# First expert rows of a token written plainly with the residual; no base rows stored, no spare products ahead of the first gathered rows

## The chip, the cores and the metric

The kernel runs on one core of one Trainium2 chip. The metric is device time in microseconds (us) of one execution, as a median of several. Engines: TensorE (PE, with its weight loads shown as PEld), VectorE (DVE), ScalarE (ACT), GpSimd (POOL) and SyncE (SP), whose queue only issues transfers. Sixteen DMA engines carry the transfers of all queues.

## The reference, cut to what matters

One encoder layer on 768 tokens (512 + 256) of width 1024, in fp32. A token mixer gives h; then a mixture of experts is added to it: 32 experts in 4 groups, one group for each token, and two experts of that group.

```
h = x + token_mixer(rms_norm(x))
gp = softmax(x @ w_group_router + b);  g_val, g_idx = top_k(gp, 1)
ep = softmax(el[group g_idx]);         e_val, e_idx = top_k(ep, 2)
gate = g_val * e_val / sum(e_val)
for e in range(32):
    hdn = silu(x @ w_gate[e]) * (x @ w_up[e])
    y = y + combine[:, e:e+1] * (hdn @ w_down[e])
return h + y
```

Here x in the second part is rms_norm(h). Each expert has 3 x 256 x 1024 weights, 3 MB in fp32, so the 32 experts bring 96 MB from memory. Each token has exactly two expert rows, so 1536 rows of 4 KB are gathered and 1536 rows are brought to the output.

## The kernel before

**Projection and routing.** After attention the kernel goes through six tiles of 128 tokens. For each tile TensorE does the output projection, DVE adds the residual (`residual`), which leaves the tile of h in `h_sb`, and the router runs: logits, the two experts (columns 182 and 183 of `route_f`), weights, and the place of each token in the slot list of each expert. Every tile of h is stored twice: by ACT's queue into the table `token_rows`, from which the experts gather (`store_row`), and by SP's queue into the output `out`, as the base to which expert rows are added (`store_h`). Before POOL gathers anything it waits for both. SP's queue issues the loads of the experts' weights between these stores.

**Slots.** For each tile TensorE multiplies a one-hot matrix (`slot_a`) by a table with three blocks of 32 columns (`slot_b`: token number, gate weight, rstd), `slot_product`. This gives for each pair of experts and each slot which token it holds, or a number beyond the last token for an empty slot. The first 64 tokens of an expert lie in block 0 (`idx_all`, `gate_all`), the next 64 in block 1 (`idx_more`, `more_all`).

**Pairs.** Experts j and j+16 make pair j, 0 to 15, with 64 slots each, so 128 rows. For each pair POOL gathers the rows by an indirect DMA (`gather_pair`, two pairs ahead, three buffers `g_rows`), TensorE transposes them, multiplies by gate and up weights (`gate_up`, L884), ACT and DVE make `hid`, TensorE transposes and multiplies by the down weights (`down`, L900), ACT copies one half of the product to `y_sb` and DVE the other half (`y_copy`), and POOL adds the 128 rows to `out` by an indirect DMA that adds at its destination (`add_rows`, L1702). Entries of an empty slot lie out of bounds and move nothing. The next add starts when the one before has landed (`main.added`). The last pair adds two halves of its rows (`add_half`, L1708). An expert with more than 64 tokens needs a further pass on the same weights (`over`, block 1); pair 0 and pair 6 have one each in the profile. Within a pass for `over`, TensorE waits until its product has left the banks before it goes on to the next pair, and POOL waits until its add has landed before it gathers again.

**Weights.** SP's queue keeps three buffers of pair weights (6 MB each) filled (`load_pair`, `refill`): a part of pair j is loaded once pair j-3 has used its buffer (waits on `g_mm`, `gu_mm`, `y_mm`) and the third transfer before it has landed (`part_in`). Pair 3's gate weights have a buffer of their own.

**Ahead of the first pair** TensorE issues 40 products that nobody reads (`keep_clock(40)`, L823), then transposes the first gathered rows (L871).

All pairs run in one order written out by hand on every engine: pairs 0 to 3, a loop over 4 to 12, pairs 13 to 15 (`run_pairs`).

## Time and profile before

| what | value |
|---|---|
| median of 3 runs | 608.5 us (605.67 to 611.92) |
| the profiled execution's own time | 608.44 us |
| its span, first to last instruction | 606.7 us |
| mean granted TensorE clock | 0.967 of 2.4 GHz |
| PE busy / DVE busy / ACT busy / POOL busy | 536.3 / 218.0 / 168.9 / 139.8 us |
| moved by DMA | 140.97 MB |

The time of the execution is 1.7 us more than its span. Busy times are sums over stages with different limits; a matmul counts as busy while it is in the pipeline, so 88% for PE does not say that PE sets the time everywhere. In the profile a transfer's share is given of all sixteen DMA engines together.

### The profile page before, as it was taken

The page shows a single profiled execution, that of the slowest core. Times are in us where ns is not written, and L with a number is a line of the kernel's source. Part 1 is how long each engine was busy: PE and PEld are TensorE (multiplying, and loading weights), DVE is VectorE, ACT ScalarE, POOL GpSimd, SP SyncE. Part 2 cuts the span into 40 slices and gives each one's busy share as a digit, 9 for nine tenths or more (in the row PEclk, how much of TensorE's full clock was granted, in tenths as well). Part 3 has the DMA queues.
Part 4 walks back from the last instruction along what each step waited for, and adds up shares of the span by engine and source line. Part 5 has one row for each costly group of instructions (what it writes and reads, how often), then busy time and mean ns, then how long its engine had stood idle before and what let it go on. Part 6 is the DMA issues. An engine that isn't in the chain of part 4 may idle for free.

```text
span 606.7 us, 9491 instructions
## 1 busy us (share of the span) xinstructions
PE 536.3 (88%) x3304; PEld 393.1 (65%) x3305; DVE 218.0 (36%) x602; ACT 168.9 (28%) x421; POOL 139.8 (23%) x230
## 2 busy tenths in 40 slices
PE   4899999999989999999978888878987699897794
PEld 4888988987557677788867545555644456554451
DVE  4754234333657755427772112202111112211111
ACT  6743343332434333125431201202111012111010
POOL 0232232222503300004535022222211222222212
PEclk9999999999989999999987999999998979998978
DMA  8741000012312111199979689999999999999993
GB/s 339 269 116 36 19 18 1 19 51 77 111 63 97 42 36 36 35 357 421 398 263 303 223 264 368 361 365 378 360 372 384 411 393 375 375 354 382 372 392 56
DMA packets 33458, 140.97 MB, mean 232 GB/s; under 512 B 10489, under 2 KB 11148, under 8 KB 21351
## 3 DMA queue, kind: packets, MB, share of 16 engines
q1 hardware_dynamic: 25776, 124.33, 53.6%
q0 software_dynamic: 5856, 12.60, 8.7%
q10 hardware_dynamic: 1766, 3.25, 1.4%
q8 instruction: 36, 0.59, 0.4%
q14 instruction: 24, 0.19, 0.1%
HBM read 131.15 MB, written 16.46 MB: 243 GB/s over the span
## 4 chain that ended last, share of the span: by engine, by line
DMA 36%; PE 16%; DVE 2%; issue 2%; ACT 1%; POOL 0%; SPq 0%; ACTq 0%; DVEq 0%; POOLq 0%
DMA expert_w<-in_w_gate 17%; DMA expert_w<-in_w_up 17%; PE ps L884 5%; PE ps L900 2%; DMA token_gates<-gate_rows 2%; PE ps L795 2%; PE ps L521 1%; PE ps L522 1%; PE ps L526 1%; PE ps L780 1%; PE ps L823 1%; PE ps L769 1%; PE ps L912 1%; POOL out L1708 0%; PE ps L871 0%
## 5 line engine op out<-in xcount | busy, mean ns | idle before, releaser
L884 PE MATMUL ps<-expert_w,xT 128*64 128x256 f32 x1120 | 128.5, 387 | 15.2 <-issue 5.6
L884 PEld LDWEIGHTS ps<-expert_w,xT 128*64 128x64 f32 x1120 | 93.7, 140 | 53.4 <-issue 23.5
L900 PE MATMUL ps<-expert_w,hT 128*64 128x512 f32 x272 | 66.6, 633 | 17.2 <-DVE hT L1546 16.0
L1702 POOL DMA_INDIRECT out<-y_sb,idx_now x17 | 27.2, 1597 | 161.2 <-issue 85.2
L1539 DVE SCALAR_TENSOR_TENSOR hid<-s_act,gate,ps 128x256 f32<-128x256 f32 x18 | 12.0, 665 | 140.1 <-ACT s_act L1171 140.1
L900 PEld LDWEIGHTS ps<-expert_w,hT 128*64 128x64 f32 x272 | 22.5, 145 | 50.7 <-issue 48.5
L1171 ACT ACTIVATE s_act<-ps,gate 128x256 f32<-128x256 f32 x18 | 8.5, 473 | 132.1 <-PE ps L884 132.1
L521 PE MATMUL ps<-w_in_hi,aT_hi 128*128 128x384 f32 (+2 forms) x120 | 43.7, 369 | 0.0
L522 PE MATMUL ps<-w_in_lo,aT_hi 128*128 128x384 f32 (+2 forms) x120 | 40.8, 345 | 0.0
L1551 DVE COPY y_sb<-ps 128x512 f32<-128x512 f32 x18 | 12.4, 692 | 76.3 <-PE ps L900 70.8
L1176 ACT ACTIVATE y_sb<-ps 128x512 f32<-128x512 f32 x18 | 10.7, 597 | 80.0 <-PE ps L900 74.6
L1074 ACT ACTIVATE p_sb<-ps,a_stat 128x512 f32<-128x512 f32 (+1 forms) x24 | 14.8, 616 | 55.9 <-DVE a_stat L1355 55.5
L871 PE MATMUL ps<-consts_sb,g_rows 128*128 128x128 f32 x128 | 19.6, 297 | 8.1 <-DMA g_rows<-token_rows,idx_now 6.2
L1165 ACT ACTIVATE xT<-ps,g_x 128x128 f32<-128x128 f32 x72 | 20.5, 368 | 20.2 <-PE ps L871 20.2
L871 PEld LDWEIGHTS ps<-consts_sb,g_rows 128*128 128x128 f32 x128 | 16.2, 196 | 14.1 <-DMA g_rows<-token_rows,idx_now 7.1
L526 PE MATMUL ps<-w_in_hi,aT_lo 128*128 128x384 f32 (+2 forms) x120 | 24.3, 344 | 0.0
L522 PEld LDWEIGHTS ps<-w_in_lo,aT_hi 128*128 128x128 f32 x120 | 22.6, 188 | 2.7 <-issue 1.2
L521 PEld LDWEIGHTS ps<-w_in_hi,aT_hi 128*128 128x128 f32 x120 | 22.6, 188 | 2.7 <-issue 1.2
L526 PEld LDWEIGHTS ps<-w_in_hi,aT_lo 128*128 128x128 f32 x120 | 20.6, 188 | 1.6
L627 PE MATMUL ps<-w_ukv_sb,cT_kv 128*128 128x512 f32 x48 | 21.6, 592 | 0.0
L641 PE MATMUL ps<-kT,qT 128*128 128x512 f32 (+1 forms) x48 | 20.9, 560 | 0.0
L521 PE MATMUL ps<-w_out_hi_o,o_hi 128*128 128x512 f32 x48 | 19.8, 413 | 1.0 <-DVE route_f L1377 1.0
(229 smaller groups left out, 944.1 us busy)
## 6 DMA issues: line engine op xcount, KB each, us to landing
expert_w<-in_w_up SPq DMA_DIRECT2D x32, 1024.0 KB, 10.0
expert_w<-in_w_gate SPq DMA_DIRECT2D x30, 1024.0 KB, 9.3
expert_w<-in_w_down SPq DMA_DIRECT2D x30, 1024.0 KB, 9.6
w_in_raw<-in_w_in SPq DMA_DIRECT2D x8, 608.0 KB, 8.6
w_out_raw<-in_w_out SPq DMA_DIRECT2D x8, 512.0 KB, 4.1
token_rows<-h_sb ACTq DMA_DIRECT2D x6, 512.0 KB
out<-h_sb SPq DMA_DIRECT2D x6, 512.0 KB, 11.3
x_sb<-in_x_prompt SPq DMA_DIRECT2D x4, 512.0 KB, 10.7
```

The source lines that it names most:

```text
L521: pe.matmul(dst, l_hi(k), r_hi(k), start=(first and k == ks[0]), stop=False)
L522: pe.matmul(dst, l_hi(k), r_lo(k), start=False, stop=False)
L526: mm = pe.matmul(dst, l_lo(k), r_hi(k), start=False, stop=(last and k == ks[-1]))
L627: mm = pe.matmul(ps[:, 5 + n, :], cT_kv[:, k, :], w_ukv[:, k, n * 512:(n + 1) * 512], start=(k == 0), stop=(k == KKV - 1))
L641: pe.matmul(ps[:, bank + u, 0:n], qT[:, h, q], kT[:, h, keys], start=True, stop=False)
L871: mm = pe.transpose(ps[:, banks + k // 4, (k % 4) * P:(k % 4 + 1) * P], blocks[:, k, :], ident)
L884: mm = pe.matmul(ps[r, GU_BANK[q.o], g * FH:(g + 1) * FH], xT[:, q.o, k, r], w_gu(j, b, lane, k, g), start=(k == 0), stop=(k == KD - 1))
L900: mm = pe.matmul(ps[r, 4 + half, :], hT[:, q.o, k, r], w_dn(b, lane, k, half), start=(k == 0), stop=(k == 1))
L1074: act.activation(p_sb[:, w % 4, 0:n], ps[:, 2 * (m % 2) + u, 0:n], ACT.Exp, bias=a_stat[:, w % 4, 1:2], scale=SCALE, accum_out=a_stat[:, w ...
L1165: ins = act.activation(xT[:, q.o, k, :], ps[:, bank, k * P:(k + 1) * P], ACT.Copy, scale=g_x[:, k:k + 1])
L1551: dve.tensor_copy(y_sb[:, buf, 512:1024], ps[:, 5, :]).then_inc(q.y_dve, 1)
L1702: pool.indirect_dma_start(out=out, out_offset=bass.IndirectOffsetOnAxis(ap=idx, axis=0), in_=y_sb[:, buf, :], in_offset=None, compute_op=A ...
```

## The change

1. **Base rows.** The six stores of h to `out` are gone, and so is the store of zeros to its 128 spare rows and POOL's wait for them. SP's queue issues the loads of pair 1 right behind those of pair 0.
2. **First rows.** Of a token's two experts, the one with the lower number comes first in the order of pairs. For it the row of h is added on chip, and the sum is written plainly, not added: DVE computes `y_sb = g_rows * first + product` over all 1024 columns in one instruction (`y_rows`), reading both banks; `first` is 1 or 0 per slot. ACT no longer copies the product, except in the last pair, which stays as it was.
3. **Two transfers for one.** Each pass is brought out by two indirect DMAs on POOL (`put_rows`): a plain one with the slots where `first` is 1, and an adding one with the rest; the entries of the other kind lie out of bounds in each. Waits on `added` count 32 for a pass instead of 16.
4. **Making `first`.** Two DVE comparisons per tile, a fourth block of columns in `slot_b` (two more small ACT instructions per tile; slot products 128 columns wide instead of 96), four more small POOL instructions per tile for the gate table, and on DVE six small instructions for the two index tables `put_all` and `put_more` ahead of pair 0.
5. **Gathering.** POOL's gather for pair j+2 waits for DVE's `y_rows` of pair j-1 where it waited for TensorE's transposes, since the gathered rows are now read once more.
6. **Spare products.** `keep_clock(40)` is left out; `keep_clock(8)` further ahead stays.

```diff
-            def store_h(i):
-                sp.wait_ge(h_done, 2 * (i + 1))
-                sp.dma_start(out[i * P:(i + 1) * P, :], h_sb[:, i, :]).then_inc(h_stored, 16)
-
             load_pair(sp, 0, 0)
-            store_h(0)
-            load_pair(sp, 1, 1, range(3))
-            store_h(1)
-            load_pair(sp, 1, 1, range(3, 6))
-            for i in range(2, NT - 1):
-                store_h(i)
+            load_pair(sp, 1, 1)
             sp.wait_ge(o_mm, 2 * NT)
-            store_h(NT - 1)
...
             more_slots(last)
-            keep_clock(40)
...
                 def closing(n):
                     hidden_transposes(over, n)
-                    pe.wait_ge(main.y_act, j + 1)
+                    if last:
+                        pe.wait_ge(main.y_act, 1)
                     pe.wait_ge(main.y_dve, j + 1)
                     down(over, b, n)
-                    pe.wait_ge(over.y_act, n + 1)
                     pe.wait_ge(over.y_dve, n + 1)
...
                 for c in range(2):
-                    ins = act.activation(slot_b[:, i % SLOT_BUFS, c, 1, :], R[:, 224 + E * c:224 + E * (c + 1)], ACT.Copy,
-                                         scale=R[:, 410 + c:411 + c])
+                    for n, at in ((1, 410), (3, 412)):
+                        ins = act.activation(slot_b[:, i % SLOT_BUFS, c, n, :], R[:, 224 + E * c:224 + E * (c + 1)], ACT.Copy,
+                                             scale=R[:, at + c:at + c + 1])
...
+            def put_rows(idx, factors, put):
+
+                first = factors[:, :, 2]
+                dve.scalar_tensor_tensor(out=put[:, :, 1], in0=first, scalar=2.0 * NO_TOKEN, in1=idx[:, 0:PAIRS], op0=ALU.mult, op1=ALU.add)
+                link("route", route_step, dve.tensor_scalar(put[:, :, 0], first, -2.0 * NO_TOKEN, 2.0 * NO_TOKEN, ALU.mult, ALU.add))
+                dve.tensor_tensor(put[:, :, 0], put[:, :, 0], idx[:, 0:PAIRS], ALU.add).then_inc(idx_done, 1)
...
+            def y_rows(q, n, buf, rows, g):
+
+                dve.wait_ge(q.y_mm, n + 1)
                 y_free(dve, q, n)
-                dve.tensor_copy(y_sb[:, buf, 512:1024], ps[:, 5, :]).then_inc(q.y_dve, 1)
+                dve.scalar_tensor_tensor(out=y_sb[:, buf, :].rearrange("t (n f) -> t n f", n=2), in0=rows.rearrange("t (n f) -> t n f", n=2),
+                                         scalar=gate[:, g, 2:3], in1=ps[:, 4:6, :], op0=ALU.mult, op1=ALU.add).then_inc(q.y_dve, 1)
...
-            def add_rows(q, n, buf, idx):
-                pool.indirect_dma_start(out=out, out_offset=bass.IndirectOffsetOnAxis(ap=idx, axis=0),
+            def put_rows(q, buf, g):
+                pool.indirect_dma_start(out=out, out_offset=bass.IndirectOffsetOnAxis(ap=idx_put[:, g, 0:1], axis=0),
+                                        in_=y_sb[:, buf, :], in_offset=None,
+                                        bounds_check=T - 1, oob_is_err=False).then_inc(q.added, 16)
+                pool.indirect_dma_start(out=out, out_offset=bass.IndirectOffsetOnAxis(ap=idx_put[:, g, 1:2], axis=0),
                                         in_=y_sb[:, buf, :], in_offset=None, compute_op=ALU.add,
                                         bounds_check=T - 1, oob_is_err=False).then_inc(q.added, 16)
...
                     if not (isinstance(j, int) and j == 0):
-                        pool.wait_ge(main.x_tr, j)
+                        pool.wait_ge(main.y_dve, j)
                     gather_pair(j + 2, (b + 2) % 3, 2 * j + 1)
...
-                    waits = [(idx_set, add_count(j)), (main.y_act, j + 1), (main.y_dve, j + 1)]
+                    waits = [(idx_set, 2 * j + 2), (main.y_dve, j + 1)]
                     if not (isinstance(j, int) and j == 0):
-                        waits.append((main.added, 16 * j))
+                        waits.append((main.added, 32 * j))
                     ready(*waits)
-                    add_rows(main, j, b, idx_now[:, 3 + b:4 + b])
+                    put_rows(main, b, b)
```

Where the instructions stand. On POOL, in the loop over pairs, from the copy of the indices to the end of a further pass (`idx_now` and `idx_put` hold the indices; 896x1024 is `out`), before:

```order
L1694 COPY idx_now<-idx_all 128x1
L1702 DMA out<-y_sb,idx_now 896x1024 [waits main_added,main_y_dve,idx_set,main_y_act]
L1774 COMPARE_AND_BRANCH
L1775 COMPARE_AND_BRANCH
L1776 UNCONDITIONAL_BRANCH
L1776 ISA
L1702 DMA out<-y_sb,idx_now 896x1024 [waits main_added,more_y_act,more_y_dve]
```

and after:

```order
L1776 COPY idx_put<-put_all 128x2
L1707 DMA out<-y_sb,idx_put 896x1024 [waits main_added,idx_set,main_y_dve]
L1710 DMA out<-y_sb,idx_put 896x1024
L1789 COMPARE_AND_BRANCH
L1790 COMPARE_AND_BRANCH
L1791 UNCONDITIONAL_BRANCH
L1791 ISA
L1707 DMA out<-y_sb,idx_put 896x1024 [waits main_added,put_set,more_y_dve]
L1710 DMA out<-y_sb,idx_put 896x1024
```

Each pass has a second indirect DMA right behind the first, with no wait of its own; it stands ahead of the next pair's gather.

On TensorE, between the last slot products and the first pair (`m_sum` is the tile's mask, L871 or L857 the transposes of the first gathered rows), before:

```order
L795 MATMUL ps<-slot_b,slot_a 128x64 [waits slot_b_done,idx_done]
L795 MATMUL ps<-slot_b,slot_a 128x64
L857 MATMUL ps<-m_sum,bf_consts 128x32 [waits pos_done]
L795 MATMUL ps<-slot_b,slot_a 128x96 [waits slot_a_done,idx_done]
L795 MATMUL ps<-slot_b,slot_a 128x96
L795 MATMUL ps<-slot_b,slot_a 128x96 [waits slot_a_done]
L795 MATMUL ps<-slot_b,slot_a 128x96
L823 MATMUL ps<-bf_consts 128x128 x40
L871 MATMUL ps<-consts_sb,g_rows 128x128 [waits counts_done,main_gathered0]
L871 MATMUL ps<-consts_sb,g_rows 128x128 x7
```

and after:

```order
L782 MATMUL ps<-slot_b,slot_a 128x96 [waits slot_b_done,idx_done]
L782 MATMUL ps<-slot_b,slot_a 128x96
L844 MATMUL ps<-m_sum,bf_consts 128x32 [waits pos_done]
L782 MATMUL ps<-slot_b,slot_a 128x128 [waits slot_a_done,idx_done]
L782 MATMUL ps<-slot_b,slot_a 128x128
L782 MATMUL ps<-slot_b,slot_a 128x128 [waits slot_a_done]
L782 MATMUL ps<-slot_b,slot_a 128x128
L857 MATMUL ps<-consts_sb,g_rows 128x128 [waits counts_done,main_gathered0]
L857 MATMUL ps<-consts_sb,g_rows 128x128 x7
```

The 40 products between the slot products and the first transposes are gone, and the slot products are wider.

## Rows read from the trace of the kernel before

**Rows 1.** Page, part 3 (queue: packets, MB, share) and part 6 (issues, landing in us)

```profile
q0 software_dynamic: 5856, 12.60, 8.7%
...
out<-y_sb,idx_now POOLq DMA_INDIRECT x17, 10.1
...
g_rows<-token_rows,idx_now POOLq DMA_INDIRECT x15, 11.0
```

**Rows 2.** Chain that ended last, in order of time: start us, us, what

```profile
361.49 7.87 DMA expert_w<-in_w_gate
...
570.89 3.67 PE ps L884 x32
```

**Rows 3.** Busy time by stretch: us, PE, PEld, DVE, ACT, POOL, PEclk, DMA share, GB/s

```profile
361.00:571.00 210.00, 176.66 (x1264) 111.01 (x1262) 34.53 (x69) 30.95 (x84) 44.20 (x60) 0.97 1.01 376
```

**Rows 4.** DMA queues from 260 to 302 us (42 us)

```profile
q10 hardware_dynamic: 885, 2.22, 13.8%
q0 software_dynamic: 178, 0.00, 0.4%
```

**Rows 5.** DMA queues in four stretches: 353 to 369, 445 to 465, 465 to 485, 525 to 545

```profile
q0 software_dynamic: 288, 0.46, 19.9%
...
q0 software_dynamic: 144, 0.52, 13.0%
...
q1 hardware_dynamic: 1081, 7.91, 94.5%
...
q1 hardware_dynamic: 814, 5.90, 79.2%
```

**Rows 6.** ACT ahead of pair 0: start us, us, engine, line, instruction [idle before <-releaser]

```profile
319.29 5.82 ACTq L1118 DMA_DIRECT2D token_gates<-gate_rows  x2
325.14 1.28 ACT L1156 ACT_TABLE_LOAD   x1 [6.38 <-DMA token_gates<-gate_rows]
...
326.97 1.14 ACT L1165 ACTIVATE xT<-ps,g_x 128x128 f32<-128x128 f32 x4 [0.33 <-PE ps L871]
```

**Rows 7.** TensorE ahead of pair 0

```profile
322.50 3.48 PE L823 MATMUL ps<-bf_consts 128*128 128x128 bf16 x40
325.82 1.11 PE L871 MATMUL ps<-consts_sb,g_rows 128*128 128x128 f32 x8
328.16 7.13 PE L884 MATMUL ps<-expert_w,xT 128*64 128x256 f32 x64 [1.23 <-ACT xT L1165]
```

**Rows 8.** Busy time by stretch, two stretches (columns as in rows 3)

```profile
324.00:325.00 1.00, 1.00 (x14) 1.00 (x13) 0.42 (x4) 0.00 (x0) 0.00 (x0) 0.61 0.25 98
...
490.00:492.00 2.00, 2.00 (x8) 0.76 (x6) 0.00 (x0) 0.00 (x0) 0.00 (x0) 0.50 1.04 432
```

**Rows 9.** TensorE, transposes of pair 9 after a wait

```profile
485.06 1.97 PE L871 MATMUL ps<-consts_sb,g_rows 128*128 128x128 f32 x8 [4.88 <-DMA g_rows<-token_rows,idx_now]
```

**Rows 10.** DVE in pair 0 and its further pass

```profile
351.51 0.41 DVE L1546 COPY hT<-ps 128x256 f32<-128x256 f32 x1
355.88 0.69 DVE L1551 COPY y_sb<-ps 128x512 f32<-128x512 f32 x1 [3.95 <-PE ps L900]
```

**Rows 11.** POOL and TensorE: further pass of pair 0, then pairs 8 to 11

```profile
359.51 1.56 POOL L1702 DMA_INDIRECT out<-y_sb,idx_now  x1 [5.29 <-DMA out<-y_sb,idx_now]
...
369.87 1.09 POOL L1683 DMA_INDIRECT g_rows<-token_rows,idx_now  x1 [0.90 <-POOL idx_now L1694]
...
379.11 1.16 PE L871 MATMUL ps<-consts_sb,g_rows 128*128 128x128 f32 x8 [1.31 <-DMA g_rows<-token_rows,idx_now]
...
495.63 1.60 POOL L1702 DMA_INDIRECT out<-y_sb,idx_now  x1 [11.89 <-issue]
...
498.35 1.09 POOL L1683 DMA_INDIRECT g_rows<-token_rows,idx_now  x1 [0.91 <-POOL idx_now L1694]
...
509.06 1.60 POOL L1702 DMA_INDIRECT out<-y_sb,idx_now  x1 [8.88 <-issue]
...
514.01 1.17 PE L871 MATMUL ps<-consts_sb,g_rows 128*128 128x128 f32 x8
```

More of the change, by code:

```diff
@@ L324, in y_free @@
         def y_free(eng, q, n):
-            if q is over:
-                if not (isinstance(n, int) and n == 0):
-                    eng.wait_ge(over.added, 16 * n)
-            elif not (isinstance(n, int) and n < 3):
-                eng.wait_ge(main.added, 16 * (n - 2))
+            if q is main and not (isinstance(n, int) and n < 3):
+                eng.wait_ge(main.added, 32 * (n - 2))
         def pT_copy(eng, m, u):
@@ L1196, in pair @@
                     x_copy(main, j + 1)
[L1197 to L1198 removed]
+                else:
+                    y_copy(j, b)
+                rest_passes(todo, lambda n: None, opening)
             x_copy(main, 0)
```

107 lines of the change are left out of this document (59 added, 48 removed).

## Prediction

> **What bounds the kernel now.** I read the chain of work that ended last first, in order of time. Up to 361.5 us it runs over TensorE, DVE and ACT. From 361.49 to 570.89 every piece of it is a load of gate or up weights, one behind the other; then come TensorE and the last two adds [rows 2]. The windows of that stretch say the same: the sixteen DMA engines are busy 1.01 of 210 us at 376 GB/s [rows 3]. PE is busy 177 us there, but waits seldom, because a pair takes it 13.4 us when it runs freely (the adds at 495.63 and 509.06 [rows 11]), while the loads take 19 us a pair (pairs 4 to 14 in 209 us [rows 2]). So the end is: the time at which the load of pair 4 starts, plus the work of the DMA engines until 571, plus a tail of 36 us (606.7 less 570.9). Three questions follow: what the change does to the start, to the DMA work, and whether TensorE stays ahead.
>
> **The start (up to 361.5).** The six stores of h lie in a stretch in which TensorE is busy throughout, so taking them away frees transfers that nobody waits for: I count 0. The loads of pair 1 end some 8 us earlier (3.1 MB at the rate of that stretch) and pair 2 still waits for the last projection. Of the small instructions, the four on POOL per tile (1.6 us) and the two on ACT (0.5 us) have idle time ahead of their readers in tiles 0 to 4; only behind the last tile are they on the path. There: two DVE comparisons in tile 4 and two in tile 5, of which one pair is ahead of ACT's `slot_b`, and two more ACT instructions of 0.26 us. ACT then issues the gate store, waits for the one before to land, loads its table and starts the copy of the first transposed rows at 326.97, which lets `gate_up` begin at 328.16 [rows 6, 7]. The table load ends at 326.42 and a tiny instruction follows it, so that ACT waits for the transposes for 0.33 us only [rows 6]: more than that, leaving out 3.48 us of products cannot gain. The added instructions move ACT's side by 0.35 (DVE) and 0.53 (ACT), from 326.64 to 327.5, so the copy starts 0.6 us later than at 326.97, with the products gone: +0.6. The six index instructions on DVE (about 1.4 us) end with the transposes; I count 0, at most +1.
>
> **The clock.** The granted clock was at half (1.2 GHz) during most of the spare products and rose around 324.6 [rows 7, 8], so before the change all of `gate_up` ran at 2.4 GHz. Now TensorE has about 1 us of nothing, transposes at half clock (1.97 us [rows 9] instead of 1.11), a gap, and then `gate_up`. The nearest row is pair 9: after a wait of 4.88 us the transposes start at half clock at 485.06, and at 492 it is still half, 7 us of thin work later [rows 8, 9]. From 325 that makes 332, so `gate_up` (from 328.7) has 3.3 us at half clock and loses 1.7 us. Bounds: 0, if the transposes and the slot products ahead count as continuous work; 3.5, if all 7.13 us run at half clock. I take 1.7.
> The Trainium skill ("TensorE: Matmul & The Clock Gate", What's actually happening) says that the throttled state is the default, that activity releases it, and that the ramp costs under 1% of a typical span. It speaks against leaving the products out; its bound would allow up to 6 us here instead of 1.7. The trace agrees with the two levels, 0.50 and 1.00.
>
> **Bringing rows out of pair 0.** DVE takes 0.41 us for 256 and 0.69 for 512 columns [rows 10], 1.1 ns each, so 1.25 us for 1024: +0.56. In an ordinary pair TensorE reads those banks again 13 us later and the difference is hidden. In pair 0 with its further pass it is not: hT of the further pass stands behind it on DVE, and TensorE waits for the second one before pair 1. That is 2 x 0.56 = +1.1. In pair 6 the same +1.1 falls while TensorE has slack. Sum of the start: 0.6 + 1.7 + 1.1 = **+3.4 us**.
>
> **The DMA work.** An added row: 445 to 465 holds one adding pass of nearly full slots, 0.52 MB = 127 rows, 13.0% of 20 us of 16 engines = 41.6 us, 0.328 us per row [rows 5]. A plain row: the tile stores on ACT's queue, 2.22 MB = 542 rows in 13.8% of 42 us of 16 engines, 0.171 us [rows 4]. Difference 0.157 us. Every token has one first row, 768 in all (the software queue's 12.60 MB are 1536 rows each way [rows 1]); those of pair 0 and its further pass, 112 rows (0.46 MB [rows 5]), go out ahead of or at the start of the bound stretch. 656 x 0.157 / 16 = **-6.4 us**.
> Against it stand the added entries: 16 passes from there on, each with 128 more entries and 16 semaphore writes, mostly out of bounds. The trace shows no such DMA by itself. Lower bound: the 4-byte scatters, 178 packets in 0.4% of 42 us, 15 ns each [rows 4], so 16 x 144 x 15 ns / 16 = 2.2 us. Upper bound: the two adds from 353 to 369, 50.9 us of engine time less 112 rows at 0.328, over 176 small packets, 80 ns each [rows 5], so 11.5 us. The lower one is measured under load, as here, the upper one in a window with little else to do; I take **+2.2**.
> Weights move at 2.39 us per MB of share while few rows are added and at 2.68 in another window (94.5% of 20 us for 7.91 MB; 79.2% for 5.90) [rows 5]. If the adds made all of this difference of 0.29 and half of them went, the 69 MB of the stretch would gain 10 us; if they made half of it, 5. I count 0, since the two windows differ in gathers too.
> Sum: -6.4 + 2.2 = -4.2 us.
>
> **Does TensorE stay ahead?** POOL's second DMA costs 1.1 us and a gap of 0.3. In pair 0 the further pass can go out only when both have landed, and the next gather only when the further ones have: 359.51 and 369.87 become about 362.5 and 374.5 (start 2.9 later, two gaps of 1.4, little for landing, as pair 0 has only first rows) and the gathered rows land at 383.6 where TensorE wants them at 381.2: its wait grows from 1.31 [rows 11] to 2.4 us. Behind pair 6 the wait of 4.88 us [rows 9] grows to some 8. By this TensorE starts pair 9 at 502 instead of 493.6 and pair 15 (6 x 13.4 later) at 583, where the weights let it start before at 585 and now at 584. So the two meet just at the end. I count 0, but this is where the rival lies. In the tail, TensorE may avoid one stretch at half clock, or not; 0.
>
> **The sum** is made against the profiled execution: 608.44 + 3.4 - 4.2 = 607.6. The profiled execution lies within 0.1 us of the median of the runs before (608.5), so nothing has to be shifted, and I give **607.5 us**: no change that a measurement tells.
>
> **Rivals.**
> A, slower: *the gather comes too late.* From pair 8's copy to pair 10's transposes there are 19.4 us: POOL 1.05, add issued to gather issued 2.7 (495.63 to 498.35), landing 11.0 [rows 1], and 4.6 us of slack before 514.01 [rows 11]. The new DMA takes 1.4 of it by its issue, DVE 0.56, and the queue ahead of the gather grows by 144 entries. If these delay landing by more than 2.6 us, TensorE waits in each pair of the stretch from 490 on; if they cost as much as a pass of their own behind another (up to 6 us), it is (6 - 2.6) / 2 = 1.7 us for each of the 6 pairs, 10 us, of which 8 reach the end: 616. It decides at 2.6 us. For it: landings of 10 to 11 us show how slow this queue is beside the weights. Against it: most of the new entries move nothing. Chance 0.12.
> The Trainium skill ("DMA: Bandwidth & Descriptors", Queues, rings and completion order) says that an engine goes round between its queues and drains a packet of several entries from one before it turns to the next. By this, entries that move nothing still wait for turns behind weights; it is why the chance is not smaller.
> B, slower: *empty entries cost 80 ns.* Then 608.4 + 3.4 - 6.4 + 11.5 = 617. Chance 0.08.
> C, faster: *weights run better with half the adds.* With 5 to 10 us more gained, 597.6 to 602.6, about 600. For it: 465 to 485 against 525 to 545. Against it: the stretch before 302, with as many writes as now, shows that writes don't hurt, but not that adds do.  Chance 0.22.
> D: *the time of an add is waiting, not work*, and others use the engine meanwhile. Then nothing is saved: 608.4 + 3.4 + 2.2 = 614. Against it: shares add up to 1.01, with and without adds. Chance 0.08.
> That the change doesn't do what it says would show as an unchanged number of added rows; the tables are plain arithmetic, so I give it nothing.
>
> **How the numbers follow.** Forecast 0.5, A 0.12, B 0.08, C 0.22, D 0.08. What a measurement tells from no change is about 1%, 6 us: 602.4 and 614.5. Faster: most of C and 0.04 of the forecast, 0.22. Slower: A, B and a little of D, 0.21. Within: 0.57. The range reaches to C's middle and to A, 600 to 616; it leaves out the far half of C (0.08) and B (0.08).
>
> **What would show it.** In the changed profile the chain should run over weights again, from about 365 to 570; ACT's first copy should start near 327.5; the clock should be half in part of pair 0's `gate_up`, to 332; the DVE instruction should take 1.25 us; the software queue's share should fall from 8.7% to about 8%; TensorE's transposes should wait for rows twice only. Waits on gathered rows in every pair would mean A; a share above 9%, B; a share of the weights below 2.45 us per MB, C. Most likely to make me wrong: the share of the adds in the weights' speed, and the clock.

## The result, and the profile after

The changed kernel takes 625.6 us (median of 4, 624.2 to 626.3) against 607.4 us for the kernel before (605.7 to 611.9): 1.0285 of it, 95% interval 1.0224 to 1.0346. That is slower by 18 us, outside the range of the prediction (600 to 616).

The page of the changed kernel first: granted clock and DMA share in 40 slices, then queues, then the chain that ended last.

```profile
PEclk9999999999999999999969979979998959979998
DMA  8720100202503101499486569999999986999943
...
q1 hardware_dynamic: 24880, 120.66, 50.0%
q0 software_dynamic: 8304, 12.62, 7.4%
...
q14 instruction: 35, 0.29, 0.1%
...
DMA 27%; PE 21%; issue 6%; DVE 2%; POOL 1%; ACT 1%; DVEq 0%; POOLq 0%; ACTq 0%; SPq 0%
```

The software queue did what was foreseen: 7.4% of 624.3 is 46.2 us of engine time, where 8.7% of 606.7 was 52.8 [rows 1]. But the DMA engines have gaps in slices 21 to 23 and 32 to 33, counted from 0 (328 to 374 and 499 to 531 us), and the chain is no longer one load behind the other all the way [rows 2]. So not the transfers but something that holds them back has to be found. I laid the starts of `gate_up` of each pair side by side. The changed kernel is 1.7 us behind at pair 1, 11.4 at pair 2, about 16 at pairs 7 and 8, 25.8 at pair 9, 30.4 at pair 12, and 17.6 at the end: loss comes at two places. The first is pair 1. TensorE there, in the kernel before (start us, us, engine, line, instruction, idle before and its releaser):

```profile
357.47 7.13 PE L884 MATMUL ps<-expert_w,xT 128*64 128x256 f32 x64 [1.75 <-DVE y_sb L1551]
```

and in the changed one (the view ends at 384 us, so its last line is cut short there):

```profile
338.42 7.13 PE L870 MATMUL ps<-expert_w,xT 128*64 128x256 f32 x64 [1.42 <-DVE xT L1520]
...
359.14 2.77 PE L870 MATMUL ps<-expert_w,xT 128*64 128x256 f32 x23 [2.18 <-DVE y_sb L1549]
365.24 7.67 PE L870 MATMUL ps<-expert_w,xT 128*64 128x256 f32 x41 [3.33 <-issue]
...
382.12 2.16 PE L870 MATMUL ps<-expert_w,xT 128*64 128x256 f32 x18 [2.71 <-issue]
```

In the middle of `gate_up` of pair 1 TensorE stands for 3.33 us with no releaser ("issue"), and then runs at half clock. By stretch (columns as in [rows 3]; PEclk is the number ahead of the DMA share):

```profile
362.00:365.00 3.00, 0.00 (x0) 0.00 (x0) 0.00 (x0) 0.00 (x0) 0.05 (x1) 0.89 0.62 231
365.00:368.00 3.00, 2.76 (x14) 1.62 (x16) 0.00 (x0) 0.00 (x0) 0.19 (x1) 0.50 0.03 5
```

Three of the small terms are seen as forecast: the half clock in the first transposes (1.97 us, as in [rows 9]) and in part of `gate_up` of pair 0, which takes 8.50 us where it took 7.13 [rows 7], and the longer instruction of DVE (L1549; 0.69 us for half of it in [rows 10]). ACT's first copy is not: it starts at 326.23, and 327.5 was forecast.

```profile
323.65 1.97 PE L857 MATMUL ps<-consts_sb,g_rows 128*128 128x128 f32 x8 [0.60 <-DMA g_rows<-token_rows,idx_all]
327.41 8.50 PE L870 MATMUL ps<-expert_w,xT 128*64 128x256 f32 x64 [1.80 <-ACT xT L1152]
```

```profile
326.23 1.13 ACT L1152 ACTIVATE xT<-ps,g_x 128x128 f32<-128x128 f32 x4
```

```profile
351.54 1.28 DVE L1549 SCALAR_TENSOR_TENSOR y_sb<-g_rows,gate,ps 128x1024 f32<-128x1024 f32 x1 [3.84 <-PE ps L886]
```

The second place is pair 9, where TensorE waited 4.88 us for gathered rows [rows 9]. The same place after:

```profile
510.64 1.97 PE L857 MATMUL ps<-consts_sb,g_rows 128*128 128x128 f32 x8 [14.50 <-DMA g_rows<-token_rows,idx_now]
```

POOL ahead of it, before: the add of pair 6, that of its further pass, the index copy and the gather for pair 9:

```profile
452.63 1.60 POOL L1702 DMA_INDIRECT out<-y_sb,idx_now  x1 [17.65 <-issue]
465.83 1.58 POOL L1702 DMA_INDIRECT out<-y_sb,idx_now  x1 [11.60 <-DMA out<-y_sb,idx_now]
475.37 0.18 POOL L1694 COPY idx_now<-idx_all 128x1 int32 x1 [7.96 <-issue]
476.48 1.08 POOL L1683 DMA_INDIRECT g_rows<-token_rows,idx_now  x1 [0.93 <-POOL idx_now L1694]
```

and after (L1707 is the plain put, L1710 the adding one, L1688 the gather):

```profile
468.37 1.02 POOL L1707 DMA_INDIRECT out<-y_sb,idx_put  x1 [16.67 <-issue]
469.69 1.59 POOL L1710 DMA_INDIRECT out<-y_sb,idx_put  x1 [0.31 <-issue]
481.32 1.01 POOL L1707 DMA_INDIRECT out<-y_sb,idx_put  x1 [10.04 <-DMA out<-y_sb,idx_put]
482.64 1.55 POOL L1710 DMA_INDIRECT out<-y_sb,idx_put  x1 [0.30 <-issue]
498.41 0.19 POOL L1699 COPY idx_now<-idx_all 128x1 int32 x1 [14.22 <-issue]
503.95 1.07 POOL L1688 DMA_INDIRECT g_rows<-token_rows,idx_now  x1 [5.35 <-issue]
```

The pieces of the chain say what is in these 14.22 and 5.35 us (start, us, what):

```profile
482.64 8.88 DMA out<-y_sb,idx_put
...
492.48 5.68 issue
...
498.44 0.17 POOL idx_now L1699
498.65 4.49 issue
...
503.95 6.64 DMA g_rows<-token_rows,idx_now
510.64 1.99 PE ps L857 x8
```

So the gather stands behind two landings in series (10.0 and 8.9 us) and behind two stretches of 5.68 and 4.49 us in which GpSimd waits for nothing the trace shows. The landings are not what is new: the kernel before waits for two as well, 13.2 us from put to put and 10.65 from the second put to the gather; after it is 12.95 and 22.63. Of the 12 us more in the second part, 10.2 are the two stretches and 1.3 is the second transfer. TensorE frees no weight buffer meanwhile, no load is issued from 502 to 519.7 us, and the DMA engines run dry:

```profile
500.00:520.00 20.00, 8.58 (x34) 4.32 (x36) 1.38 (x3) 1.14 (x4) 5.30 (x7) 0.57 0.61 207
```

That is 0.61 of 20 us, where the kernel before had 1.02. One clue names a resource. There are two queues of kind "instruction" in the profile. One, q8, carried 36 transfers in both kernels; the other, q14, carried 35 against 24 before. Between 480 and 555 us q14 had none before, and now:

```profile
q1 hardware_dynamic: 3178, 23.13, 77.0%
q0 software_dynamic: 1753, 2.45, 11.9%
q14 instruction: 8, 0.07, 0.2%
```

Five of these eight fall into stretches in which GpSimd stands: at 496 and 501 us, inside the two named above (492.5 to 498.2 and 498.6 to 503.1), and at 539, 540 and 545 us, inside the idle time ahead of the next late gather (issued at 547.77, after which pair 12 waits 2.79 us for its rows).

Theory: engines stand while their instructions are fetched, and the changed code is laid out so that this happens more often. Rivals: the two transfers per pass in series; the work of the queue; the clock.

### The profile page after: what moved, and what is told of

Its sections match the earlier page's. It is cut to its first block, busy times and chain, and to the rows that moved or that the text cites. A ratio compares the mean times of both kernels' runs of the same rounds, so it can differ in the third digit from the quotient of the medians.

```text
span 624.3 us, 9452 instructions
## 1 busy us (share of the span) xinstructions
PE 534.7 (86%) x3264; PEld 389.9 (62%) x3265; DVE 229.6 (37%) x620; ACT 162.0 (26%) x416; POOL 163.8 (26%) x274
## 4 chain that ended last, share of the span: by engine, by line
DMA 27%; PE 21%; issue 6%; DVE 2%; POOL 1%; ACT 1%; DVEq 0%; POOLq 0%; ACTq 0%; SPq 0%
PE ps L870 10%; DMA expert_w<-in_w_down 9%; PE ps L886 6%; DMA expert_w<-in_w_up 6%; DMA out<-y_sb,idx_put 3%; DMA expert_w<-in_w_gate 3%; DMA token_rows<-h_sb 3%; DMA token_gates<-gate_rows 2%; DMA g_rows<-token_rows,idx_now 1%; PE ps L508 1%; PE ps L509 1%; PE ps L513 1%; PE ps L767 1%; DVE xT L1520 1%; ACT s_act L1158 1%
## 5 line engine op out<-in xcount | busy, mean ns | idle before, releaser
L870 PE MATMUL ps<-expert_w,xT 128*64 128x256 f32 x1120 | 133.3, 397 | 20.9 <-issue 9.0
L1707 POOL DMA_INDIRECT out<-y_sb,idx_put x17 | 17.3, 1019 | 144.7 <-DVE y_sb L1549 66.2
L1549 DVE SCALAR_TENSOR_TENSOR y_sb<-g_rows,gate,ps 128x1024 f32<-128x1024 f32 x15 | 19.2, 1281 | 62.3 <-PE ps L886 58.3
L857 PE MATMUL ps<-consts_sb,g_rows 128*128 128x128 f32 x128 | 21.0, 314 | 17.9 <-DMA g_rows<-token_rows,idx_now 17.3
L857 PEld LDWEIGHTS ps<-consts_sb,g_rows 128*128 128x128 f32 x128 | 17.3, 199 | 24.1 <-DMA g_rows<-token_rows,idx_now 18.2
L1710 POOL DMA_INDIRECT out<-y_sb,idx_put x17 | 26.9, 1584 | 5.2 <-issue 5.2
L1688 POOL DMA_INDIRECT g_rows<-token_rows,idx_now x15 | 16.1, 1072 | 22.9 <-issue 12.0
```

Source lines behind the costliest of these rows:

```text
L857: mm = pe.transpose(ps[:, banks + k // 4, (k % 4) * P:(k % 4 + 1) * P], blocks[:, k, :], ident)
L870: mm = pe.matmul(ps[r, GU_BANK[q.o], g * FH:(g + 1) * FH], xT[:, q.o, k, r], w_gu(j, b, lane, k, g), start=(k == 0), stop=(k == KD - 1))
L1549: dve.scalar_tensor_tensor(out=y_sb[:, buf, :].rearrange("t (n f) -> t n f", n=2), in0=rows.rearrange("t (n f) -> t n f", n=2), scalar=gat ...
L1688: pool.indirect_dma_start(out=dst, out_offset=None, in_=src, in_offset=bass.IndirectOffsetOnAxis(ap=idx, axis=0), bounds_check=T - 1, oob_ ...
L1707: pool.indirect_dma_start(out=out, out_offset=bass.IndirectOffsetOnAxis(ap=idx_put[:, g, 0:1], axis=0), in_=y_sb[:, buf, :], in_offset=Non ...
L1710: pool.indirect_dma_start(out=out, out_offset=bass.IndirectOffsetOnAxis(ap=idx_put[:, g, 1:2], axis=0), in_=y_sb[:, buf, :], in_offset=Non ...
```

## The experiments

Each stands beside runs of the kernel before on the same chip; ratios are to it. "Short code" means that GpSimd's code for a third and later pass of a pair is left out; with these inputs no expert has so many rows (more than 128 of them; the "256 rows in a lane" of one expectation below is wrong), so that code is never run. It is a kernel for such inputs only. In the compiled programs GpSimd's loop over pairs 4 to 12, three turns of three pairs, is 303 instructions long before (of 1335), 369 after (of 1554). Where instruction transfers are counted below, they are those of q14.

**Spare products back.**

```diff
+            keep_clock(40)
```

> The changed kernel with the 40 spare products ahead of the first gathered rows put back, nothing else. In the changed kernel TensorE stalls at two places where no semaphore is shown as the releaser: 3.33 us in pair 1 (at 365.24 us, after which the granted clock is 0.50 until 371) and 2.71 us before pair 2 (at 382.12), and the kernel is 11.4 us behind the kernel before when pair 2 begins, while it was only 1.7 behind at pair 1. Theory L (the stalls of TensorE come from where its instructions lie in the stream, and leaving out the spare products shifted them): the stall in pair 1 and the half clock after it are gone or lie elsewhere, pair 2 begins 6 to 10 us earlier, and the end comes 3 to 9 us earlier, about 617 to 622 us; the later stalls of GpSimd stay. Theory C (the clock ahead of pair 0): gate_up of pair 0 takes 7.1 us again and not 8.5, and all else stays: 624 to 625 us. Theory S (stalls on GpSimd alone made it slower, the stall in pair 1 is one of its gathers' consequences): no change beyond 1.5 us.

Measured: 619.9 us, 1.0232 (1.014 to 1.0324). The stall in pair 1, its half clock and the stall ahead of pair 2 are gone, the wait of pair 9 is still there:

```profile
360.90 7.13 PE L871 MATMUL ps<-expert_w,xT 128*64 128x256 f32 x64 [2.12 <-DVE y_sb L1550]
...
504.85 1.97 PE L858 MATMUL ps<-consts_sb,g_rows 128*128 128x128 f32 x8 [14.83 <-DMA g_rows<-token_rows,idx_now]
```

Pair 2 begins at 374.12 us and not at 382.12. Theory L fits by the trace; the times agree (5.7 us between the medians) without proving it, as the interval takes in 1.0285. C falls by the trace, and S with the stall gone. The other instruction queue, q8, moved at the same place; that it is TensorE's is an inference, from its transfers and TensorE's stalls alone. In pairs 0 and 1 the kernel before and this one have a transfer on it at about 343. In the changed kernel none came between 333 and 362, and the stall ends 3 us after that one; in the kernel with GpSimd's loop written out (below) it is one at 365 and a stall that ends at 367.98.

**Short code on GpSimd**, by itself and with the spare products.

```diff
-                    with pool.If(todo > 1):
-                        with pool.Fori(1, todo) as p:
-                            n = pool.snap(before)
-                            more_add(j, n)
-                            more_gather(j, p + 1)
-                            pool.reg_add(before, before, 1)
```

> The changed kernel without the code on GpSimd for a third and later pass of a pair (experts with more than 256 rows in a lane); with these inputs that code is never run, so the same instructions are executed, but GpSimd's program is some 450 instructions shorter (1105 against 1554), and the other engines' by about 40. Theory F (instruction fetch: the loop over pairs on GpSimd became about 70 instructions longer and is fetched anew at each jump, which stalled GpSimd for 4 to 14 us after the further passes, so that gathered rows of pairs 9 and 12 came late): the transfers on the instruction queue fall from 35 to 27 or fewer, the waits of the row transposes for gathered rows at 510 us (14.50) and 556 us (2.79) shrink to under 5 us in all, and the time is 8 to 16 us shorter, 610 to 617 us. Theory D (two transfers for each pass land later than one, whatever the code): instruction count changes nothing, 623 to 626 us. Theory W (work of the DMA engines and clock): the same, 623 to 626 us.

> The changed kernel with both edits of the two kernels above: 40 spare products put back on TensorE, and GpSimd's never-run code for a third and later pass left out. Theory F with theory L: the two gains add up, nearly all of the 18 us goes, 605 to 611 us, and the start of each pair is within 3 us of the kernel before. Theory F alone: as the kernel with the shorter GpSimd code. Theories D and W: 622 to 625 us.

Measured: 611.9 us, 1.0101 (1.0056 to 1.0146), and with both edits 610.4 us, 1.0101 (1.0012 to 1.019). The instruction queue has 22 transfers and none from 480 to 555 us; with both edits pair 9 waits 6.19 us:

```profile
493.27 1.97 PE L858 MATMUL ps<-consts_sb,g_rows 128*128 128x128 f32 x8 [6.19 <-DMA g_rows<-token_rows,idx_now]
```

Code that is never run costs 14 us by the medians (625.6 to 611.9), 11 by the ratios, by being there: theories D and W fall as the main cause. The time of both edits is at the edge of what F with L forecast, but the two gains did not add up, and 1% is left. The profiles of these two are of their fastest executions (605.2 and 605.0 us, spans of 603), so they don't show what the slower ones lost.

**Longer loop in the kernel before**, with 24 memsets, then with 7 gathers, in each copy of the branch that is never run.

```diff
                     with pool.If(todo > 1):
+                        for _ in range(24):
+                            pool.memset(neg_half[:, :], -0.5)
```

> The kernel before with 24 memsets put into each copy of GpSimd's never-run branch for a third pass, nothing else: the loop over pairs is 72 instructions longer on GpSimd, as it is in the changed kernel, and what is executed is the same as in the kernel before. Theory F (instruction fetch on GpSimd): more transfers on the instruction queue than the 24 of before, issue stalls of 4 us or more on GpSimd in the loop, and 3 to 15 us slower than before, 611 to 623 us. Theories D and W (what is executed counts, not its length): 607 to 609 us, no difference from before.

> The kernel before with seven gathers put into each copy of GpSimd's never-run branch for a third pass, nothing else: its loop over pairs is 366 instructions long by the compiled program (303 before, 369 in the changed kernel), and what is added are indirect transfers, as in the changed kernel, and not memsets, as in the kernel with the padding of memsets, which was as fast as the kernel before (0.9996). What is executed is the same as in the kernel before. Theory F2 (instruction fetch decides, and an indirect transfer takes more room in the stream than the compiled program shows, so the padding with memsets did not reach the length from which the loop is fetched anew each time): transfers on the instruction queue between 480 and 540 us, where before had none, stalls of 4 to 5 us on GpSimd at the start of the loop, 3 to 15 us slower than before. Theory X (what is executed decides, and the kernel with the short code gained by its missing jumps and not by fetches): no difference from before, within 3 us.

Measured: 607.0 us, 0.9996 (0.9958 to 1.0035), and 605.2 us, 0.9965 (0.9925 to 1.0004); 25 and 24 instruction transfers, none from 480 to 540 us. Theory F as I had put it, that the length of the loop decides, was wrong: loops of 375 and 366 instructions do no harm there.

**Short code in the kernel before** (the edit as above).

> The kernel before with the same cut as made the changed kernel 14 us shorter: GpSimd's code for a third and later pass of a pair, never run with these inputs, is left out; the residual and base rows are stored and everything is added, as before. If the shorter code helps every version alike, before becomes 8 to 14 us faster too (594 to 600 us), and the change by itself costs 10 us or more. If it only takes away what the change had brought (theory F2: the loop before was short enough already, it had no transfers on the instruction queue in 480 to 540 us), it stays within 3 us of before, 605 to 611 us, and the change by itself costs 2 to 4 us.

Measured: 606.1 us, 0.9981 (0.9945 to 1.0018). So the edit takes away only what the change had brought.

**GpSimd's loop over pairs written out**, in the changed kernel and in the one before.

```diff
+            if eng.engine == nc.gpsimd.engine:
+                for j in range(PAIRS):
+                    pair(j, j // 3, j % 3, j == PAIRS - 1)
+                return
             for j in range(4):
```

> The changed kernel with GpSimd's loop over the pairs 4 to 12 written out, so that its program has no jump backwards from pair to pair (2135 instructions against 1554); all other engines keep theirs, nothing is left out. Theory F2: instructions come in the order in which they lie, so the stalls at the loop's head (5.4 us before the gathers at 503.95 and 547.77) go, though the long jumps over code that is not run stay; 8 to 16 us faster than the changed kernel, 610 to 617 us. If every new instruction has to be fetched at a price wherever it lies (theory G), the stalls spread over all pairs: as the changed kernel or slower, 623 us or more.

> The kernel before with GpSimd's loop over the pairs written out in the same way (1811 instructions against 1335). Its loop had no transfers on the instruction queue from 480 to 555 us, so by theory F2 there is little to gain: 604 to 609 us. By theory G its later pairs have to be fetched, which they were not before: 3 us or more slower.

Measured: 615.9 us, 1.016 (1.0084 to 1.0237), and 607.6 us, 0.998 (0.9944 to 1.0017). Against the changed kernel that is a gain by the medians; the intervals just meet (1.0237 and 1.0224). Instructions in sequence cost nothing that shows; jumping back to code that has to be fetched does, as the next experiment shows. The rest of the changed kernel's loss is in its trace: 3.31 us of stall in pair 1 again, and 6.79 for the rows of pair 9.

**The loop moved, not changed**: memsets in the never-run branch of pair 0 alone, 64 or 128 of them.

```diff
                     with pool.If(todo > 1):
+                        if isinstance(j, int) and j == 0:
+                            for _ in range(64):
+                                pool.memset(neg_half[:, :], -0.5)
```

> The changed kernel with 64 memsets in GpSimd's never-run branch of pair 0 alone: its loop over pairs keeps its 369 instructions and its code, but begins 64 instructions later in the program (961 and not 897). Nothing else is changed and the same is executed. Two kernels whose loop is as long (375 and 366) did not fetch theirs anew, so length is not what decides. Theory P (what decides is where the loop lies against the blocks in which instructions are fetched): of the shifts by 64 and by 128 at least one takes the transfers on the instruction queue between 480 and 550 us away (9 in the changed kernel) and makes it 8 to 16 us faster, 610 to 617 us. Theory Q (what is executed in the loop decides, that is more instructions run through in each turn, wherever it lies): both shifts as the changed kernel, 623 to 627 us.

> As the kernel above with a shift of 128 instructions (the loop begins at 1025). Theory P: if the blocks are 128 instructions long, this shift changes nothing (623 to 627 us) and the one by 64 may; if they are 256 long, this one lies as far as can be from the present place and helps: 610 to 617 us. Theory Q: 623 to 627 us.

Measured: by 64, 614.8 us, 1.0095 (1.0057 to 1.0133); by 128, 628.4 us, 1.034 (1.0291 to 1.0389). The loop has the same 369 instructions and runs the same ones; moved by 64 it has 25 instruction transfers, none of them from 480 to 555 us, and pair 9 has no wait of over 1 us; moved by 128 it has 36 transfers, eight of them from 480 to 555 us, and this:

```profile
510.47 1.97 PE L857 MATMUL ps<-consts_sb,g_rows 128*128 128x128 f32 x8 [14.26 <-DMA g_rows<-token_rows,idx_now]
```

This is the cleanest pair of the study. The place of the loop decides, and a shift by 128 instructions is as none: that is 8 KB at the 64 bytes that an instruction takes in the compiled program, the mean size of a transfer on that queue (0.29 MB in 35). The trace doesn't say which engine a queue of instructions serves; what ties this one to GpSimd is that its transfers and GpSimd's stalls come and go together. POOL at the same place, moved by 64; 1.08 us from the index copy to the gather, where the changed kernel had 5.54:

```profile
479.97 1.01 POOL L1707 DMA_INDIRECT out<-y_sb,idx_put  x1 [5.40 <-DMA out<-y_sb,idx_put]
481.29 1.55 POOL L1710 DMA_INDIRECT out<-y_sb,idx_put  x1 [0.30 <-issue]
486.45 0.19 POOL L1699 COPY idx_now<-idx_all 128x1 int32 x1 [3.61 <-issue]
487.53 1.07 POOL L1688 DMA_INDIRECT g_rows<-token_rows,idx_now  x1 [0.90 <-POOL idx_now L1699]
```

The times and the transfers carry this conclusion, not the size of the gap in this one trace: from the first put behind pair 6 to the gather it is 15.9 us here and 35.6 in the changed kernel, and only 10.2 of the 19.7 us between them are the stalls. The rest is that both landings were shorter here (idle 5.40 and 3.61 us ahead of the second put and the copy); why, no run shows.

The Trainium skill ("Runtime: NRT & Kernel Launch", Instruction fetch mechanics) says that prefetch is sequential and that a taken branch to a target outside the present two-page window has to fetch it first. The traces agree with such a stall (transfers at 496 and 501 us, GpSimd standing around both); the page's blocks of 256 instructions would let a shift by 128 matter, which it did not here.

**The same shift in the kernel before.**

> The kernel before with 64 memsets in GpSimd's never-run branch of pair 0, nothing else: its loop (303 instructions) begins at 860 and not 796. In the changed kernel this same shift took the transfers on the instruction queue between 480 and 550 us away. Theory P: a loop of 303 instructions fits the store in nearly every place, as that of 366 and of 375 in the other two places, so no difference: 604 to 610 us. If even the short loop can be thrown out by its place, fetches appear from 480 to 555 us and it is 5 us or more slower, above 612 us.

Measured: 606.7 us, 1.0017 (0.9988 to 1.0046), 24 instruction transfers. I found no place at which the shorter loop is hit; two were tried.

**What is left of the loss.** Two edits on the kernel with spare products and short code. First, every pass's adding transfer left out, so that the second expert's rows don't reach the output:

```diff
-                pool.indirect_dma_start(out=out, out_offset=bass.IndirectOffsetOnAxis(ap=idx_put[:, g, 1:2], axis=0),
-                                        in_=y_sb[:, buf, :], in_offset=None, compute_op=ALU.add,
-                                        bounds_check=T - 1, oob_is_err=False).then_inc(q.added, 16)
```

> The kernel with both edits (spare products back, GpSimd's third pass left out; 1.0101 of before) without the second, adding transfer of every pass: only the first expert's rows of each token are written, what a token's second expert and shared pairs add is left out, so less is computed into the output. What is left of the loss against before, some 6 us in the measured ratio, can come from the two transfers of each pass, which land one after the other in front of the next gathers, or from the longer step on VectorE and the start. Theory D (two transfers): half the transfers of this queue's stores are gone, the wait of the row transposes of pair 9 (6.19 us at 493.27) falls under 4 us, the kernel is 3 us or more faster than the one with both edits, 601 to 607 us. Theory Y (VectorE's step and the start): no gain beyond 2 us, 608 to 612 us.

Second, GpSimd's wait for the further pass's landing moved from right behind it to the next use of what it guards:

```diff
                 put_rows(over, 3, 3)
-                pool.wait_ge(over.added, 32 * (n + 1))
...
+            def landed():
+                with pool.If(pool.snap(before) > 0):
+                    ready((over.added, 32 * pool.snap(before)))
...
                 with pool.If(todo > 0):
+                    landed()
                     pool.tensor_copy(idx_now[:, 6:7], idx_more[:, bass.ds(j, 1)]).then_inc(more_set, 1)
...
                     ready(*waits)
+                    if not (isinstance(j, int) and j == 0):
+                        landed()
                     put_rows(main, b, b)
```

> The kernel with both edits, in which GpSimd no longer waits for the landing of a further pass's two transfers before it goes on to the next pair: the wait stands ahead of the next transfers into the output and ahead of the next further gather, so the gather of the pair after next is issued some 9 us earlier after a further pass. Theory D (landings in series hold back the gathers): the wait of pair 9's transposes (6.19 us in the kernel with both edits) is gone, and the time is 2 to 6 us shorter, 604 to 608 us. If the transfers' landing hides under the weights anyway (theory Y): 608 to 612 us. It has more branches on GpSimd (12 more in the loop), which may cost what it gains.

Measured: without the adding transfers 598.7 us, 0.9844 (0.9795 to 0.9892); with the moved wait 602.1 us, 0.9893 (0.9842 to 0.9945). Both have no wait for rows in pair 9. Theory Y falls. The first edit proves less than the second, since it takes away the work of the adding transfers along with their landing. The moved wait leaves nothing out of the transfers and gains 2.1% against the same kernel without it, by intervals that don't meet (0.9842 to 0.9945 against 1.0012 to 1.019); it is 1% faster than the kernel before. Neither kernel has an instruction transfer from 480 to 555 us, so the gain is not one of fetches there. So what was left of the loss goes with the wait for a landing that stands ahead of a gather. That rests on the times: the kept profile of the kernel with both edits is of its fastest execution, and its chain runs over loads from 375 to 565 us in spite of a wait of 6.19 us for the rows of pair 9.

**Is that the change's gain or the moved wait's?** The moved wait and the short code in the kernel before:

> The kernel before with the cut of GpSimd's third pass and with the wait for the landing of a further pass's transfers moved behind the next gather, as in the kernel with both edits and this one (0.9893 of before). It tells what the change itself is worth once neither the place of the loop nor that wait stands in its way: the kernel with the change and the moved wait against the same without the change. Theory G1 (the change gains what its transfers save, some 5 us of DMA work, once the gathers are early): before with the moved wait stays within 3 us of before, 605 to 609 us, so the change is worth 4 to 6 us there. Theory G2 (all of the gain is the moved wait's): before gains as much, 600 to 603 us, and the change is worth nothing.

Measured: 607.3 us, 1.0022 (0.9997 to 1.0046). The moved wait brings the kernel before nothing: its chain from 513 to 567 us is again one load behind the other. So, in this form, the change is worth 0.9893 / 1.0022 = 0.987, some 8 us (roughly 0.981 to 0.993, from the two intervals). Where from is seen in the queues between 420 and 560 us (packets, MB, share), without the change, then with it:

```profile
q1 hardware_dynamic: 6400, 46.61, 82.6%
q0 software_dynamic: 2880, 6.64, 18.8%
```

```profile
q1 hardware_dynamic: 6742, 49.09, 86.3%
q0 software_dynamic: 4011, 6.17, 15.0%
```

The software queue's share falls by 3.8 points of 140 us, 5.3 us, and the weights take it up: 2.48 MB more, 5%. The weights' own price hardly moves: 0.826 x 140 / 46.61 = 2.48 us per MB without, 2.46 with the change.

**All of it in one, with nothing left out**: the changed kernel with spare products, moved wait and GpSimd's loop written out in place of the short code (the diffs above; the third pass keeps its wait).

> The changed kernel with nothing left out of it: 40 spare products back, the wait for the landing moved, and GpSimd's loop over the pairs written out in place of the cut, so that experts of any size are still served. By the theory that place of the loop, stall of TensorE in pair 1 and serial landings were the whole loss, it is as fast as the kernel with the cut and the moved wait, 600 to 605 us, faster than both kernels of the case. If the written-out code has fetches of its own in the way (the written-out changed kernel still had a wait of 6.8 us for rows, which the moved wait should take), 605 to 611 us.

Measured: 601.1 us, 0.9926 (0.9897 to 0.9955): the fastest that computes everything for any size of expert, some 24 us below the changed kernel and, by the ratio, 4.5 below the one before. Its chain, in order of time, is over loads down to the last pair:

```profile
552.60 9.42 DMA expert_w<-in_w_up
562.04 8.91 DMA expert_w<-in_w_gate
570.96 8.72 DMA expert_w<-in_w_up
579.68 0.14 issue
579.82 3.69 PE ps L875 x32
```

## Why the prediction was wrong

**What bounds the kernel**: held for the kernel before. That it would go on to hold for the changed one did not.

**The start, +0.6**: the copy that carried this term started 1.3 us earlier than forecast, and the term is too small to be told in the times. `gate_up` of pair 0 begins at 327.41 us against 328.16 [rows 7]; over all profiles it begins at 327.3 to 331.5 with the change and at 326.8 to 331.2 without. The chain does run over GpSimd's instructions for the last gate row (321.0 to 324.5 us), which I had not put on the path.

**The clock, +1.7**: right for pair 0. 8.50 us instead of 7.13, so 1.4. The half clock behind the stall in pair 1 was not in the sum.

**Bringing rows out of pair 0, +1.1**: right. The instruction takes 1281 ns (forecast 1.25 us). From `gate_up` of the further pass to that of pair 1 it is 20.65 us with the spare products back, 19.69 before: +0.96.

**The DMA work, -4.2**: the right sign, too small. Over the whole execution it is 6.6 us (46.2 against 52.8). Over 420 to 560 us alone, in the kernels with the moved wait, the queue's share fell by 5.3 us, and by the same rate over the 210 us of the bound stretch it is 8. Which of its two terms was off, -6.4 for the rows or +2.2 for the empty entries, no run separates. Rivals B and D fall with that: the share of the queue is 7.4%, not above 9%, and the weights take up what is saved. Of C, only the size of the gain is met, not its reason: the price of a MB of weights did not fall. The page "DMA: Bandwidth & Descriptors" of the Trainium skill (Queues, rings and completion order), which I had weighed for A, speaks of turns between queues; no run here isolated what they cost.

**"Does TensorE stay ahead? ... I count 0"**: this step failed. Its arithmetic was sound as far as it went: it had pair 9 start at 502 us, and with both stalls removed it starts at 501.47. In that profile pair 15 starts at 583.44, where 583 was forecast. But in the changed kernel pair 9 started at 519.33, as I had costed GpSimd's and TensorE's new work by the instructions that run and took their supply as free. The runs put in its place:
- GpSimd's loop lies where its code is fetched anew when it turns back (ahead of pairs 7 and 10), with stalls of 4.5 to 5.7 us ahead of the gathers. It is worth about 11 us by the ratios (shift by 64: 1.0095, short code: 1.0101, against 1.0285). That the place of the loop decides is shown by the two shifts; that the stalls are fetches is read from the transfers inside them.
- TensorE's 3.3 us of stall in pair 1 and the half clock behind it, worth 3 us by the ratios and 6 by the medians (the spare products back: 1.0232, 619.9 us). That it hangs on leaving out the products is shown; that it is a late fetch is argued from its queue. It was also absent with short GpSimd code and no spare products, where TensorE's compiled program differs from that of the changed kernel only in 40 instructions at its very end, and present in both shifted kernels, so the place of TensorE's code is not all of it. That stays open.
- The wait for a further pass's landing ahead of a gather: moving it is worth 8 us by the medians (610.4 to 602.1) and 12 by the ratios (1.0101 to 0.9893). I had seen this one ("the wait of 4.88 us [rows 9] grows to some 8") and counted it at 0, as the weights would end it. With both edits the wait was 6.19 us, near my figure, and in that fast execution (605.0 us) the weights did end it; by the medians it was not free. The kernel before has the same wait and gains nothing when it is moved (1.0022). Why it costs one kernel and not the other stays open; what the traces show is that pair 9 starts 8 us later with both edits than before (501.47 against 493.57), so that less slack is left behind it.

These sizes overlap and do not add up: each hides part of another.

**Rival A** had the place right (gathers too late) and the direction, for another reason; its 616 us was 10 short. Its mechanism, a wait in each pair from 490 us on, did not occur: there were two waits for rows, 14.50 us in pair 9 and 2.79 in pair 12, each at a turn of GpSimd's loop.

**The chances**: 0.21 for slower was too little, and the range ended where the one step that I doubted ended. A bound taken only from what the instructions do left no room for a stall of supply. The trace of the kernel before had a stall without a releaser that I could have read, on TensorE ahead of pair 7, where its loop turns back for the first time. Whether that one is a fetch is not shown: q8 has no transfer between 440 and 460 us.

```profile
458.01 8.73 PE L884 MATMUL ps<-expert_w,xT 128*64 128x256 f32 x64 [2.33 <-issue]
```

## What to carry to other kernels

When a change adds instructions inside a loop of an engine that issues gathers, or takes a long run of instructions away ahead of one, look at the queue of kind "instruction" in both profiles and at idle time that is put down to "issue": here code that was never run decided about 2% of the time. Test it by moving the loop without changing it, and write the loop out where it matters. And when transfers get a second one behind them, look for waits that stand right behind a transfer on the engine that also issues the next gathers: with the spare products back and the short code, moving one to the first use of what it guards turned this change from a loss of 1% into a gain of 1%, though the same move gained the kernel before nothing.

## What the runs showed that I had not expected

- The same 369 instructions in a loop, moved by 128 or by 64: 36 or 25 instruction transfers, 628 or 615 us. Moved by 128 is as if not moved.
- The instruction transfers are of two sizes: 0.59 MB in 36 (16 KB) on the one queue, 0.29 MB in 35 (8 KB) on the other.
- One such stall costs GpSimd 4.5 to 5.7 us beside weight traffic. The one on TensorE, probably a fetch too, costs 3.3 us, and about as much again at half clock: 41 matrix products in 7.67 us, against 64 in 7.13.
- An adding indirect transfer takes GpSimd 1.58 us to issue, a plain one 1.02 us, whatever their rows.
